# Laying out modulation weights by 256 channels and contracting the first projection chunk in four steps

## The reference, cut to what matters

```python
def rms_norm(x, g):
    y = xf * lax.rsqrt(jnp.mean(xf * xf, axis=-1, keepdims=True) + NORM_EPS)
    return (y * g.astype(jnp.float32)).astype(x.dtype)

def first_block(x, c, positions, w_ada, b_ada, norm_pre, ..., w_in, conv_w, conv_b, ...):
        mod = jnp.einsum('bd,de->be', jax.nn.silu(c), w_ada[l]) + b_ada[l]
        shift, scale, gate = jnp.split(mod, 3, axis=-1)
        h = rms_norm(x, norm_pre[l]) * (1.0 + scale[:, None, :]) + shift[:, None, :]
        proj = jnp.einsum('bsd,de->bse', h, w_in[l])
        xa, ga, q, k, v, gb = jnp.split(proj, SPLIT_IDX, axis=-1)
        xa = causal_depthwise_conv(xa, conv_w[l], conv_b[l])
        ya = rg_lru(xa, ...) * jax.nn.silu(ga)
        ya = rms_norm(ya, norm_rec[l])
```

## Time and profile before

| | us |
|---|---|
| median of 3 executions | 1869.47 |
| lowest and highest | 1867.77, 1876.37 |
| the profiled execution | 1878.58 |
| its span, from first to last instruction | 1876.8 |
| PE busy in the span | 1717.6 (92%) |
| DVE, ACT, POOL busy | 804.7, 518.8, 109.4 |
| mean granted PE clock of the span | 0.962 of full |
| moved by DMA | 359.25 MB, mean 191 GB/s |

### The profile page before, as it was taken

The page is one execution under the profiler, slowest core; times in us unless marked ns, Lnnn a source line. Parts: engine busy times, 40 slices in busy tenths (PEclk is TensorE's granted clock), DMA queues, the critical chain, the costliest instruction groups (busy, mean ns, idle before and its releaser), DMA issues.

```text
span 1876.8 us, 37887 instructions
## 1 busy us (share of the span) xinstructions
PE 1717.6 (92%) x16822; PEld 927.4 (49%) x16822; DVE 804.7 (43%) x1484; ACT 518.8 (28%) x983; POOL 109.4 (6%) x144
## 2 busy tenths in 40 slices
PE   5999999999999999999999999999999977778786
PEld 3444566544546555556667667544454333323332
DVE  3853144656627456355654554344462211222210
ACT  3710254311127422354453341122231110101010
POOL 0000010010000000100000000000001101010100
PEclk8999989999989999999998998899999999999998
DMA  9121376351110030042221210356569999999997
GB/s 396 76 88 47 145 287 247 145 224 69 45 45 1 23 151 0 17 170 82 77 81 50 63 56 24 114 219 221 219 239 398 416 425 415 422 413 425 417 423 279
DMA packets 48360, 359.25 MB, mean 191 GB/s; under 512 B 8325, under 2 KB 8557, under 8 KB 28736
## 3 DMA queue, kind: packets, MB, share of 16 engines
q1 hardware_dynamic: 35792, 311.51, 41.2%
q0 software_dynamic: 12400, 45.27, 7.3%
HBM read 337.47 MB, written 27.32 MB: 194 GB/s over the span
## 4 chain that ended last, share of the span: by engine, by line
PE 74%; DMA 16%; ACT 4%; issue 3%; DVE 2%; POOL 0%; SPq 0%; ACTq 0%; DVEq 0%; POOLq 0%
PE psum L207 71%; DMA arena<-in_w 16%; PE psum L210 3%; ACT arena L204 3%; ACT L204 1%; DVE arena L154 1%; DVE arena L180 0%; DVE arena L164 0%; DVE arena L172 0%; DVE arena L160 0%; POOL arena L141 0%; DMA arena<-in_tok 0%; DVE arena L168 0%; DVE arena L159 0%; POOL out L149 0%
## 5 line engine op out<-in xcount | busy, mean ns | idle before, releaser
L207 PE MATMUL psum<-arena 32*32 32x16 f32 (+12 forms) x16178 | 1638.1, 304 | 145.2 <-DMA arena<-in_w 73.4
L207 PEld LDWEIGHTS psum<-arena 32*32 32x32 f32 (+5 forms) x16178 | 856.0, 135 | 876.3 <-issue 764.7
L204 ACT ACTIVATE arena<-psum 128x512 f32<-128x512 f32 (+5 forms) x334 | 171.4, 513 | 871.2 <-PE psum L207 670.7
L154 DVE TENSOR_TENSOR arena<-arena,psum 128x512 f32<-128x512 f32 (+3 forms) x128 | 64.9, 507 | 402.6 <-PE psum L207 209.2
L154 DVE TENSOR_TENSOR arena<-arena 128x512 f32<-128x512 f32 (+10 forms) x315 | 191.6, 608 | 31.0 <-ACT arena L204 14.7
L204 ACT ACTIVATE arena<-arena 128x512 f32<-128x512 f32 (+10 forms) x254 | 138.8, 546 | 177.7 <-DVE arena L154 41.9
L204 ACT ACTIVATE arena<-psum,arena 128x128 f32<-128x128 f32 (+3 forms) x221 | 111.7, 505 | 275.1 <-PE psum L210 135.5
L154 DVE TENSOR_TENSOR arena<-psum,arena 128x128 f32<-128x128 f32 (+3 forms) x116 | 47.4, 409 | 154.5 <-PE psum L207 141.3
L164 DVE SCALAR_TENSOR_TENSOR arena<-arena 128x512 f32<-128x512 f32 (+7 forms) x162 | 103.5, 639 | 14.5 <-ACT arena L204 8.1
L210 PE MATMUL psum<-arena 128*128 128x128 f32 x644 | 102.6, 291 | 6.1 <-ACT arena L204 3.2
L172 DVE RECIPROCAL arena<-arena 128x1 f32<-128x1 f32 (+4 forms) x71 | 79.1, 1113 | 63.0 <-ACT arena L204 59.2
(11 more groups left out here) (49 smaller groups left out, 177.7 us busy)
## 6 DMA issues: line engine op xcount, KB each, us to landing
arena<-in_w SPq DMA_DIRECT2D x127, 2048.0 KB, 34.5
arena<-in_w SPq DMA_DIRECT2D x48, 256.0 KB, 3.1
arena<-in_w SPq DMA_DIRECT2D x12, 1024.0 KB, 36.4
arena<-kd POOLq DMA_DIRECT2D x28, 256.0 KB, 3.4
gd<-arena SPq DMA_DIRECT2D x24, 256.0 KB, 3.2
arena<-gd SPq DMA_DIRECT2D x24, 256.0 KB, 5.6
arena<-in_w POOLq DMA_DIRECT2D x2, 2048.0 KB, 9.6
kd<-arena POOLq DMA_DIRECT2D x2, 1536.0 KB, 11.0
```

The costliest lines, as they stand in the source:

```text
L154: return self.ends(self.e.tensor_tensor(out, a, b, op))
L204: return self.ends(self.e.activation(out, a, func, **kw))
L207: return self.ends(self.e.matmul(out, lhs, rhs, start=start, stop=stop))
```

## The change

The columns of the modulation weights are regrouped when the weights are laid out: chunk j (0 to 3) holds now 256 columns of shift and the same 256 of scale, so that each chunk is enough for two slices, 2j and 2j + 1. Chunk 6, the first of `w_in`, leaves the ring and goes to a place of its own (`EB0`, which experts use at the end) in four quarters of 512 KB, each with two slices k. x comes in four transfers, one for each tile. On PE the transposes of x stand first, then row 0, columns 0, row 1, and then the four contraction steps: step j is the products of slices 2j and 2j + 1 for all four tiles of chunk 6, in four banks at once (`FIRSTBANK`), with columns j + 1 after the first tile and row j + 2 behind the step. The `lru_*` functions get t - 3 in place of t. ACT computes sine, cosine and an exponential ahead of the tiles rather than between them, and DVE the series `lru_start_vector`.

```diff
-MAIN_CHUNKS = [0, 1, 2, 3, 6, 7, 8, 9, 10, 11, 4, 5, *range(14, 24), 12, 13, 24, 25, *range(26, 34), *range(40, 45)]
+MAIN_CHUNKS = [0, 1, 2, 3, 7, 8, 9, 10, 11, 4, 5, *range(14, 24), 12, 13, 24, 25, *range(26, 34), *range(40, 45)]
...
         def pre_sync():
             Y.dma(par, T_["params"], d_par.up("par"))
             Y.dma(cst, T_["consts"], d_cst.up("cst"))
-            Y.dma(X, x_in, d_x.up("x"))
-            for c in range(4):
-                load(c)
+            for i in range(4):
+                Y.dma(X[:, i, :], x_in[:, i, :], d_x[i].up("x", i))
+            for j in range(4):
+                load(j)
+                part = slice(1024 * j, 1024 * j + 1024)
+                Y.dma(EB0[:, part], T_["w"][6][:, part], d_w6[j].up("w", 6))
 
         def pre_tensor():
-            modulation_row(0)
             for i in range(4):
                 T.wait_ge(V["n1", i])
                 turn8("f1", i, ht1[i], ALL8)
+            modulation_row(0)
+            modulation_columns(0)
             modulation_row(1)
-            modulation_columns(0)
-            modulation_row(2)
-            modulation_columns(1)
-            modulation_columns(2)
-            modulation_row(3)
-            modulation_columns(3)
+            for j in range(4):
+                T.wait_ge(d_w6[j]["w", 6], A["ht", j], V["ht", j])
+                for m in range(4):
+                    if j == 0:
+                        T.wait_ge(*ps.take(FIRSTBANK, "p1", 6, m))
+                    for k in (2 * j, 2 * j + 1):
+                        T.mm(ps["p1", 6, m], W6[:, k, c4(m)], HT[:, k, :], k == 0, k == 7)
+                    if j == 3:
+                        T.then_inc("p1", 6, m)
+                    elif m == 0:
+                        modulation_columns(j + 1)
+                if j < 2:
+                    modulation_row(j + 2)
...
-            V.wait_ge(A["f1", 3, 0])
-            for j in (2, 3):
-                columns(j)
-                o = mods[:, 4 * j:4 * j + 4]
-                V.stt(o, o, 1.0, P["npre"][:, 4 * j - 8:4 * j - 4], ALU.add, ALU.mult).then_inc("gmod", j)
-                for k in (4 * j - 8, 4 * j - 6):
-                    V.ts(HT[:, k, :], HT[:, k, :], mods[:, 8 + k:9 + k], mods[:, k:k + 1], ALU.mult, ALU.add)
-                V.then_inc("ht", j)
+            V.wait_ge(A["f1", 3, 0])
+            for j in range(4):
+                k = 2 * j
+                V.wait_ge(T["mc", j])
+                cols = ps["mc", j][:, 0:128].rearrange("p (t v) -> p t v", t=4)[:, :, 0]
+                for a, o in ((0, k), (2, 8 + k)):
+                    V.tt(mods[:, o:o + 2], cols[:, a:a + 2], P["b_mod"][:, o:o + 2], ALU.add)
+                ps.free(V.last(), "mc", j)
+                o = mods[:, 8 + k:10 + k]
+                V.stt(o, o, 1.0, P["npre"][:, k:k + 2], ALU.add, ALU.mult).then_inc("gmod", j)
+                V.ts(HT[:, k, :], HT[:, k, :], mods[:, 8 + k:9 + k], mods[:, k:k + 1], ALU.mult, ALU.add).then_inc("ht", j)
...
         def proj1_gpsimd():
-            G.wait_ge(T["w", 2])
+            G.wait_ge(T["w", 1])
...
-                lru_tensor(t)
+                lru_tensor(t - 3)
...
-                lru_scalar(t)
+                lru_scalar(t - 3)
...
-                lru_vector(t)
-                if t == 0:
-                    V.wait_ge(A["sincos"])
-                    V.ts(SIN, SIN, C["sgn"], None, ALU.mult)
-                    lru_start_vector()
+                if t > 2:
+                    lru_vector(t - 3)
...
-    parts = [(i["w_ada"][0], 8, 512), (i["w_in"][0], 8, 512), (i["w_out"][0], 8, 512), (i["w_ada_2"][0], 8, 512),
+    ada = i["w_ada"][0]
+    ada = np.concatenate([ada[:, 1024 * v + 256 * j:1024 * v + 256 * j + 256] for j in range(4) for v in range(2)] + [ada[:, 2048:]], 1)
+    parts = [(ada, 8, 512), (i["w_in"][0], 8, 512), (i["w_out"][0], 8, 512), (i["w_ada_2"][0], 8, 512),
```

More of the change, by code:

```diff
@@ L301 @@
 XBANK = (7,)
+MODBANK = (0, 1, 2, 3)
+FIRSTBANK = (4, 5, 6, 7)
 FBANK = (0, 1)
@@ L411, in dma @@
             return counts[-1]
-        d_par, d_cst, d_x, d_bias, d_lnc, d_pos, d_wbd, d_na = [
-            dma(n) for n in ("par", "cst", "x", "bias", "lnc", "pos", "wbd", "na")]
+        d_par, d_cst, d_bias, d_lnc, d_pos, d_wbd, d_na = [
+            dma(n) for n in ("par", "cst", "bias", "lnc", "pos", "wbd", "na")]
         d_mod = [dma(f"mod{i}") for i in range(3)]
@@ L420, in build @@
         d_fd = [dma("fd0"), dma("fd1")]
+        d_x, d_w6 = [dma(f"x{i}") for i in range(4)], [dma(f"w6{i}") for i in range(4)]
         d_rope, d_pw = dma("rope"), dma("pw")
@@ L604, in build @@
         EB0 = A_[:, NCOL - 4096:NCOL]
+        W6 = EB0.rearrange("p (k n) -> p k n", k=8)
         assert ar.top <= NCOL - 4096
@@ L640, in modulation_row @@
         def modulation_row(j):
-            T.wait_ge(V["cs"], W.landed(j), *ps.take(ALL8, "mr", j))
+            T.wait_ge(V["cs"], W.landed(j), *ps.take(MODBANK, "mr", j))
             modulation_blocks(ps["mr", j], wk(j), range(8))
@@ L645, in modulation_columns @@
         def modulation_columns(j):
-            T.wait_ge(A["mr", j], d_cst["cst"], *ps.take(ALL8, "mc", j))
+            T.wait_ge(A["mr", j], d_cst["cst"], *ps.take(MODBANK, "mc", j))
             T.tr(ps["mc", j][:, 0:128], mrow[j % 3], ident)
@@ L681, in pre_tensor @@
                 turn8("f1", i, ht1[i], ALL8)
+            modulation_row(0)
+            modulation_columns(0)
             modulation_row(1)
-            modulation_columns(0)
-            modulation_row(2)
-            modulation_columns(1)
-            modulation_columns(2)
-            modulation_row(3)
-            modulation_columns(3)
-        def pre_scalar():
-            def row(j):
+            for j in range(4):
[11 more added lines that the diff above has]
+                    modulation_row(j + 2)
+        def pre_scalar():
+            A.wait_ge(d_par["par"])
+            A.act(sg, par[:, 0:24], ACT.Sigmoid).then_inc("cs_sg")
+            for i in range(4):
+                A.wait_ge(d_x[i]["x", i])
+                A.act(sq1, X[:, i, :], ACT.Square, accum_out=small1[:, i:i + 1])
+            A.wait_ge(V["eps"])
+            A.act(small1[:, 12:16], small1[:, 0:4], ACT.Sqrt, bias=eps[:, 0:1], scale=1.0 / D).then_inc("sq1")
+            for i in range(4):
+                turn8_act("f1", i, HT, i)
+            for j in range(4):
                 A.wait_ge(T["w", j])
@@ L696, in row @@
                 ps.free(A.last(), "mr", j)
[L698 to L710, removed]
-            for j in (2, 3):
[L712 to L717, removed]
-        def pre_vector():
-            def columns(j):
-                o = mods[:, 4 * j:4 * j + 4]
-                V.wait_ge(T["mc", j])
-                V.tt(o, ps["mc", j][:, 0:128].rearrange("p (t v) -> p t v", t=4)[:, :, 0], P["b_mod"][:, 4 * j:4 * j + 4], ALU.add)
-                ps.free(V.last(), "mc", j)
+                k = 2 * j + 1
+                A.wait_ge(V["gmod", j], V["f1", 3, 1])
+                A.act(HT[:, k, :], HT[:, k, :], ACT.Identity, scale=mods[:, 8 + k:9 + k], bias=mods[:, k:k + 1]).then_inc("ht", j)
+        def pre_vector():
             V.zero(eps[:, 0:1], value=EPS)
@@ L738, in pre_vector @@
                 turn8_dve("f1", i, HT, i)
-            columns(0)
-            columns(1)
             V.wait_ge(A["f1", 3, 0])
-            for j in (2, 3):
-                columns(j)
-                o = mods[:, 4 * j:4 * j + 4]
-                V.stt(o, o, 1.0, P["npre"][:, 4 * j - 8:4 * j - 4], ALU.add, ALU.mult).then_inc("gmod", j)
-                for k in (4 * j - 8, 4 * j - 6):
-                    V.ts(HT[:, k, :], HT[:, k, :], mods[:, 8 + k:9 + k], mods[:, k:k + 1], ALU.mult, ALU.add)
-                V.then_inc("ht", j)
+            for j in range(4):
+                k = 2 * j
[7 more added lines that the diff above has]
+                V.ts(HT[:, k, :], HT[:, k, :], mods[:, 8 + k:9 + k], mods[:, k:k + 1], ALU.mult, ALU.add).then_inc("ht", j)
         PROJ1 = [(c, m) for c in (6, 7, 8, 9, 10, 11) for m in range(4)]
         def proj1_sync():
-            for c in (6, 7, 8, 9, 10, 11):
+            for c in (7, 8, 9, 10, 11):
                 load(c)
         def proj1_gpsimd():
-            G.wait_ge(T["w", 2])
+            G.wait_ge(T["w", 1])
             G.dma(posb, T_["positions"][0, :].partition_broadcast(128), d_pos.up("pos"))
@@ L771, in proj1_tensor @@
             for t, (c, m) in enumerate(PROJ1):
+                if t < 4:
+                    continue
                 T.wait_ge(W.landed(c), *ps.take(ALL8, "p1", c, m))
@@ L784, in proj1_tensor @@
                 late.add(rotate(c, m) if c in (8, 9) else iter(()))
-                lru_tensor(t)
+                lru_tensor(t - 3)
             late.drain()
         def proj1_scalar():
-            for t, (c, m) in enumerate(PROJ1):
[L790 to L795, removed]
+            A.wait_ge(V["lw1"])
+            A.act(lw[2], lw[1], ACT.Exp).then_inc("lw2")
+            A.wait_ge(V["ang"])
```

(6 more changed lines are left out.)

2 lines of the change are left out of this document (removed).

## The result

The changed kernel took 1878.02 us (median of 16 executions, 1872.53 to 1912.62) where the kernel before took 1868.53 (16 executions, 1862.96 to 1880.13). The ratio is 1.0043, 95% interval 1.0022 to 1.0064: **slower by 8 us**, where 10.5 us faster was forecast. That ratio leaves out executions that lie more than 1.5% above the fastest of their kernel; of the changed kernel these are 4 of 16 (1906 to 1913 us), of the kernel before none, and the profiled execution shown here is one of the four (1911.79 us, span 1910.0). A second profile of the same kernel, taken later, fell on a short execution (1878.09 us, span 1876.3), and I say where the two differ.

What follows compares the result with a forecast made beforehand. The prediction took the opening relay of transfers and PE, then gapless PE work, as the bound. An earlier projection start gave 10.9 us, taken as 10.5, from the median 1869.47 to 1859.0 us; range 1855.5 to 1865.5.

Steps and rivals of the forecast that it cites:

- S: Time at which step 0 of the projection starts on PE, forecast at 24.7 us, for a gain of 10.9 us.
- 35.6 - S: Forecast gain at the end of PE's gapless stretch, 224.7 us before, from an earlier start of step 0: 10.9 us.
- the clock one: Rival: PE's clock stays low through the opening transposes and row 0; step 0 starts at 27.6, time 1861.9 us; chance 0.27.
- short transfers do overlap: Denies the rival that split transfers of x and chunk 6 each pay a gap, up to 1885 us; chance of slower 0.04.
- Price: nothing: Recurrent branch, moved by three tiles against PE: DVE, busy 17.37 of 20 us, keeps up; cost zero.
- DVE becomes the late one: Rival: PE waits for the recurrence or a bank in tiles 4 to 11; gain 6.5 us, time 1863; chance 0.07.
- Does it arrive at the end? I count no loss: Last 450 us, held by transfers: the stream starts earlier with PE and weight buffers merely turn, so no gain is lost.
- nothing lasting: Rival: a later wait that does not move with PE takes the gain back, time 1869 us; chance 0.06.
- Stretches of low clock fall by chance, though, and spread executions by some us: Anywhere in the kernel: low clock was taken as random scatter of some us between executions.

Runs made afterwards that it cites:

- e1: The changed kernel with the turn of the eight PSUM banks moved on by four behind the projection, restoring the earlier banks; median 1868.41 us, ratio 1.0014.
- e2: The kernel before with only the turn of the eight PSUM banks moved on by four behind the projection; median 1883.01 us, ratio 1.0065.
- e4: The kernel before with three products that nobody reads put on PE between projection and attention, banks as before; median 1880.45 us, ratio 1.0026.
- e8: The kernel before with four products that nobody reads put on PE between projection and attention; median 1871.64 us, ratio 1.0011.

## Why the prediction was wrong

**"All else in the sum is S."** S itself was nearly right. The forecast had PE's first transpose at 14.2, the end of the transposes at 20.0, step 0 at 24.7. Measured in the first profile: 14.86 (x had landed at 10.99, not 10.3), 20.90, and row 1 from 23.51 with 1.96 us of work, so step 0 at 25.5. By 35.6 - S the gain is 10.1. From there on chunks 2, 3 and 7 were never waited for, the steps follow each other at 27.42 and 36.48 us in that profile without a wait, and the norm ended at 160.3, 5.8 us ahead of ACT's copy of (10, 0) at 166.10, where the prediction had 6. Of the rivals, the clock one (S = 27.6) did not occur, and short transfers do overlap: four of 512 KB for x landed in 6.7 us in the median of the DMA issues, with the share of the DMA engines at 1.01 from 14 to 50 us.

**"Price: nothing" for the recurrent branch** was the first step that failed. The rival "DVE becomes the late one", priced at 4 us with a chance of 0.07, is the nearest to it. I compared DVE's busy share (17.37 of 20) with PE's tile time and found room. The busy share doesn't contain the round trip: ACT's root, table load and copy take 2.6 us (92.79 to 95.42), of which DVE covers only 0.7 with its last product. So a round is DVE's 8.9 us of work and 1.9 of waiting, 10.9 against 8.6. The change put the gate tiles of chunk 7 into that round. Cost 2.7 us, and 1.5 more where the clock fell at the end of this wait (at 116). The gain of 10.1 became the 7.0 of the long execution, and 5.1 in the short one and 4.7 in e1, where the clock fell and the transposes had ended 0.3 and 0.7 us later; some 0.4 us are left over in each of the three.

**"Does it arrive at the end? I count no loss"** failed by an omission. The rival "nothing lasting", a later wait that takes the gain back, had 0.06 and 1869; it is what came, and it cost more than the gain. I followed what the removed chunk does to the ring of weight buffers, and not what twelve removed takes do to the ring of PSUM banks. It would have been read from the program alone: the order of the instructions is unchanged there. Cost 8.7 us of wait and about 2 of low clock, by e2 up to 12.

**"Stretches of low clock fall by chance, though, and spread executions by some us"** failed in size, and in taking for chance alone what the change itself makes more frequent. The stretch in attention is worth 33 us where it is long, and whether it is long depends on the time at which attention starts, by e4 and e8. In the new kernel a quarter of the executions have it (7 of 28), in the kernel before none of 96.

The account for executions without the long stretch: -5.1 at attention's start in the mean of the profiles, +8.7 and +2 at the ring, together +5.6, against the 8.0 of the ratio. The rest of some 2.4 us is not explained. The changed kernel lost 72.3 us to the low clock in the median and the kernel before 67.3, but the low clock at 116 and at the ring is part of these 5.0 and counted already.

## What to carry to other kernels

Where buffers or banks are handed out in turn, a removed take moves every later one: list the tenants of each bank before and after, through the whole program, or start each stage at a fixed bank. A busy share below one does not show that two engines keep up with a third; add up the round in which they wait for each other, and compare that with the third's time for a tile. And where an early saving meets a later stretch of light matrix work, the saving also moves the place at which the clock falls there; measure with the start of that stretch delayed by one, two and three products before judging the change itself.

## What the runs showed of the hardware

The granted clock in a light stretch is not a smooth risk. A delay of 2.57 us ahead of attention gave 6 of 13 executions with some 30 us more, and one of 3.43 us gave none of 12.

Transposes alone raised the clock here. In the changed kernel PE's first work is 32 transposes, and they took 6.04 us where 32 at the low clock would take 6.8 and at full speed 3.65; row 0 behind them took 1.96 us, the full-speed time of the earlier trace rows. The clock had risen when PE had done nothing but transposes. The Trainium skill, "TensorE: Matmul & The Clock Gate", Part 4, says that the full clock does not engage for them; for these float32 transposes the measurement decides against it.

A wait of 2.7 us was enough in three of the four profiles that have it for the clock to fall as it ended (at 115.4 to 116.5 us), and during the one of 8.7 us it fell in all four profiles that have it.
